# Recurrent mixer with its heads in pairs: values of two heads as one moving operand, outputs of two heads together

## The reference

```python
def _hgrn2_mixer(h, w_in, lb, out_gain, w_out):
    q, f_logit, i, g = jnp.split(h @ w_in, 4, axis=-1)
    log_f = jnp.log(lb + (1.0 - lb) * jax.nn.sigmoid(f_logit))
    k = (1.0 - lb) * jax.nn.sigmoid(-f_logit)
    ...
    _, o = lax.scan(_hgrn2_chunk, s0, (qc, kc, vc, gc))   # v is i, decay is log_f
    o = _rmsnorm(o, out_gain)
    o = o * jax.nn.sigmoid(g.astype(jnp.float32))
    return o.astype(h.dtype) @ w_out
```

## Time and profile before

| | |
|---|---|
| median of 3 runs | 1961.22 us (1957.46 to 1961.35) |
| profiled execution | 1960.82 us, its span 1958.8 us |
| PE busy | 1822.2 us, 93% |
| DVE, ACT, POOL busy | 1193.8, 959.9, 528.6 us |
| mean granted PE clock | 0.967 |
| the mixer's stage | about 226 to 430 us |

### The profile page before, as it was taken

How to read it: one execution, slowest core, us unless ns; L and a number is a source line. 1 busy time by engine, 2 the same in 40 slices (tenths; PEclk the granted TensorE clock), 3 DMA queues, 4 the chain that set the end, 5 groups by cost and what they waited for, 6 DMA issues and landing times. The chain is left out here.

```text
span 1958.8 us, 36818 instructions
## 1 busy us (share of the span) xinstructions
PE 1822.2 (93%) x14492; PEld 1787.5 (91%) x14492; DVE 1193.8 (61%) x1716; ACT 959.9 (49%) x1086; POOL 528.6 (27%) x409
## 2 busy tenths in 40 slices
PE   7999989969999899997998999979899998879999
PEld 7999879969999899996998999978799998879998
DVE  6655678866555665555666555564477763337776
ACT  5444667654435653443335444554454554445544
POOL 2001546620004500034664000565400026650001
PEclk9999989979999899998999999989999998889999
DMA  6555323225554445533343555433244543344542
GB/s 220 201 188 215 111 93 122 97 86 193 190 176 170 139 165 185 187 132 110 112 145 109 195 189 182 162 112 111 105 172 174 190 161 108 103 155 151 193 174 105
DMA packets 44877, 298.21 MB, mean 152 GB/s; under 512 B 4992, under 2 KB 5376, under 8 KB 15376
## 3 DMA queue, kind: packets, MB, share of 16 engines
q1 hardware_dynamic: 44816, 297.38, 42.7%
HBM read 296.31 MB, written 1.05 MB: 152 GB/s over the span
## 5 line engine op out<-in xcount | busy, mean ns | idle before, releaser
L2253 POOL TENSOR_TENSOR w_lo<-raw,w_hi 128x512 fp32r<-128x512 f32 (+2 forms) x403 | 527.8, 1342 | 1415.3 <-ACT w_hi L299 1415.1
L299 ACT ACTIVATE w_hi<-raw 128x2048 fp32r<-128x2048 f32 (+5 forms) x298 | 531.7, 1793 | 456.9 <-PE wk L349 374.2
L348 PE MATMUL wk<-x_lo,w_hi 128*128 128x256 f32 x2560 | 732.4, 286 | 0.0
L347 PE MATMUL wk<-x_hi,w_hi 128*128 128x256 f32 x2208 | 637.5, 289 | 27.1 <-DVE x_lo L422 15.8
L349 PE MATMUL wk<-x_hi,w_lo 128*128 128x256 f32 x2208 | 631.4, 286 | 0.0
L319 DVE TENSOR_TENSOR w_lo<-raw,w_hi 128x2048 fp32r<-128x2048 f32 x180 | 411.7, 2290 | 160.7 <-ACT w_hi L299 160.7
L348 PEld LDWEIGHTS wk<-x_lo,w_hi 128*128 128x128 f32 x2560 | 498.6, 195 | 0.4
L347 PEld LDWEIGHTS wk<-x_hi,w_hi 128*128 128x128 f32 x2208 | 430.8, 195 | 31.0 <-DVE x_lo L422 16.6
L349 PEld LDWEIGHTS wk<-x_hi,w_lo 128*128 128x128 f32 x2208 | 430.1, 195 | 0.0
L347 PE MATMUL acc<-h_hi,w_hi 128*128 128x256 f32 x1376 | 392.6, 285 | 33.5 <-DVE h_lo L2167 10.8
L348 PE MATMUL acc<-h_lo,w_hi 128*128 128x256 f32 x1376 | 387.8, 282 | 0.0
(11 more groups left out here) (294 smaller groups left out, 2258.3 us busy)
## 6 DMA issues: line engine op xcount, KB each, us to landing
raw<-w_ffn_loop SPq DMA_DIRECT2D x120, 1024.0 KB, 4.8
raw<-w_conv_loop SPq DMA_DIRECT2D x60, 1024.0 KB, 4.8
raw<-w_mla_loop SPq DMA_DIRECT2D x18, 768.0 KB, 4.2
raw<-w_hgrn_loop SPq DMA_DIRECT2D x12, 896.0 KB, 4.5
raw<-w_ple_gate SPq DMA_DIRECT2D x8, 1024.0 KB, 4.8
raw<-w_odd_loop SPq DMA_DIRECT2D x10, 768.0 KB, 4.2
raw<-w_ffn_first SPq DMA_DIRECT2D x6, 1024.0 KB, 4.8
raw<-w_even_loop SPq DMA_DIRECT2D x6, 1024.0 KB, 4.8
```

Of the source, the lines that this page charges most:

```text
L299: nc.scalar.activation(w_hi[slot][:, 0:n], raw[slot][:, 0:n], ACT.Copy).then_inc(S("hi_ready"), 1)
L347: nc.tensor.matmul(dst, hi, a_hi, start=start, stop=False, skip_group_check=True)
L348: nc.tensor.matmul(dst, hi, a_lo, start=False, stop=False, skip_group_check=True)
L2253: last = nc.gpsimd.tensor_tensor(w_lo[slot][:, a:b], raw[slot][:, a:b], w_hi[slot][:, a:b].bitcast(F32), ALU.subtract)
```

## The change

Heads are worked in pairs. The values of heads 2r and 2r+1 are projected together: `value_tiles` moves two weight tiles side by side (256 columns), 6 matmuls for two tiles. For PE and DVE there are now two bodies. The **odd** one (i = 1, 3, 5) projects f, q and g of head i+1 ahead of round a, and the values of the pair (i+1, i+2) in two halves, one behind round a and one behind round b; it has no output tiles. The **even** one (i = 2, 4, 6) projects f, q ahead of round a and g behind it, has no value tiles, and does the output tiles of both heads of the last pair, 16, behind round b. The first body has g, the first pair's values are projected ahead of it. `h_val`, `h_hi`, `h_lo`, `hg_g` and `hg_v` hold two heads. On DVE `gate` stands ahead of the gathers in the first and the odd bodies, and at the end, behind the wait for `o`, in the even ones. Units: `proj0` 40 tiles (14, 14, 12), `proj1` 24 (12, 12), a turn of the loop 80 tiles for two heads in 6 units (five of 14, one of 10).

```diff
-    def hgrn_proj(h):
-        t = [("a_w_in", k, c * D + h * P) for k in range(KD) for c in (1, 0)]
-        return t + [("a_w_in", k, c * D + h * P) for c in (3, 2) for k in range(KD)]
+    def hgrn_gates(h):
+        return [("a_w_in", k, c * D + h * P) for k in range(KD) for c in (1, 0)] + [("a_w_in", k, 3 * D + h * P) for k in range(KD)]
+
+    def hgrn_values(h):
+        return [("a_w_in", k, 2 * D + (h + n) * P) for k in range(KD) for n in range(2)]
+
+    def hgrn_out(h):
+        return [("a_w_out", h, n * P) for n in range(KD)]
...
-            mixer(name, A_HEADS, hgrn_proj, lambda h: [("a_w_out", h, n * P) for n in range(KD)],
-                  (3, 11), (3, 14), (1, 8))
+            add(name + ".proj0", 1, 3, 14, lambda i: hgrn_gates(0) + hgrn_values(0))
+            add(name + ".proj1", 1, 2, 12, lambda i: hgrn_gates(1))
+            add(name + ".loop", A_HEADS // 2 - 1, 6, 14, lambda r: hgrn_gates(2 * r + 2) + hgrn_values(2 * r + 2) + hgrn_gates(2 * r + 3)
+                + hgrn_out(2 * r) + hgrn_out(2 * r + 1))
+            add(name + ".out0", 1, 1, 8, lambda i: hgrn_out(A_HEADS - 2))
+            add(name + ".out1", 1, 1, 8, lambda i: hgrn_out(A_HEADS - 1))
...
-        HG_V_VALUES = Steps("hgrn_values", "v", "gate")
+        HG_V_VALUES = Steps("hgrn_pair_values", "v")
+        HG_V_GATE = Steps("hgrn_gates", "gate")
...
+            g_tiles = x_tiles(wk[:, 1, 0:SEQ], True)
+
+            def value_tiles(bank):
+                return x_tiles(lambda b: wk[:, bank, b * SEQ:b * SEQ + SEQ], True, tokens=True)
+
+            def body(i, kind, seg=None, first=0, pair=None):
+                has_next, has_last = kind != "last", kind != "first"
                 if has_next:
-                    use_tiles(pe, *seg, 0, f_q[:8])
+                    use_tiles(pe, *seg, first, f_q[:8])
                 if has_last:
                     mean(i - 1)
                 if has_next:
-                    use_tiles(pe, *seg, 8, f_q[8:], "hgrn_f_q_done", 15)
-                if has_next and not has_last:
-                    HG_V_VALUES.after(pe, i, "gate")
-                    use_tiles(pe, *seg, 16, x_tiles(wk[:, 1, 0:SEQ], True) + token_x)
+                    use_tiles(pe, *seg, first + 8, f_q[8:], "hgrn_f_q_done" if kind != "even" else None, first + 15)
+                if kind in ("first", "odd"):
+                    HG_V_GATE.after(pe, i, "gate")
+                    use_tiles(pe, *seg, first + 16, g_tiles, "hgrn_g_done" if kind == "odd" else None, first + 23)
                 HG_V_PREP.after(pe, i, "scaled")
                 if has_last:
                     HG_V_OUT.after(pe, i - 1, "normed")
+                else:
+                    HG_V_VALUES.after(pe, pair, "v")
                 round_(i, 0)
-                if has_next and has_last:
-                    HG_V_VALUES.after(pe, i, "gate")
-                    use_tiles(pe, *seg, 16, x_tiles(wk[:, 1, 0:SEQ], True) + token_x)
+                if kind == "odd":
+                    HG_V_GATE.after(pe, i + 1, "gate")
+                    use_tiles(pe, *seg, first + 24, value_tiles(1)[:4], wide=2)
+                elif kind == "even":
+                    HG_V_VALUES.after(pe, pair, "v")
+                    use_tiles(pe, *seg, first + 16, g_tiles)
                 if has_next:
                     HG_V_PREP.after(pe, i + 1, "q")
                 else:
                     HG_V_GATHER.after(pe, i - 1, "across")
                 HG_P_SCORES.done(nc.tensor.matmul(wk[:, 0, 0:P], kt[:, LEVELS, 0:P], qt[:, LEVELS, P:SEQ], start=True, stop=True,
                                                   skip_group_check=True), "across")
-                if not has_next:
+                if kind == "last":
                     HG_V_OUT.after(pe, i - 1, "lo")
                     use_tiles(pe, out0, 0, 0, out_tiles(1))
                 HG_V_GATHER.after(pe, i, "a3")
                 round_(i, 1)
-                if has_last and has_next:
+                if kind == "odd":
+                    use_tiles(pe, *seg, first + 32, value_tiles(1)[4:], wide=2)
+                elif kind == "even":
                     HG_V_OUT.after(pe, i - 1, "lo")
-                    use_tiles(pe, *seg, 32, out_tiles(1))
+                    use_tiles(pe, *seg, first + 24, out_tiles(2))
                 HG_V_GATHER.after(pe, i, "b3")
-                HG_V_VALUES.after(pe, i, "v")
-                nc.tensor.matmul(wk[:, 2, 0:SEQ], hg_v[:, 0:P], hg_st[:, 0:SEQ], start=True, stop=False, skip_group_check=True)
-                HG_P_O.done(nc.tensor.matmul(wk[:, 2, P:SEQ], hg_v[:, P:SEQ], hg_st[:, SEQ:384], start=False, stop=True,
+                HG_V_VALUES.after(pe, pair, "v")
+                v0, v1 = (hg_v[:, c:c + P] for c in ((0, SEQ) if kind in ("first", "even") else (P, SEQ + P)))
+                nc.tensor.matmul(wk[:, 2, 0:SEQ], v0, hg_st[:, 0:SEQ], start=True, stop=False, skip_group_check=True)
+                HG_P_O.done(nc.tensor.matmul(wk[:, 2, P:SEQ], v1, hg_st[:, SEQ:384], start=False, stop=True,
                                              skip_group_check=True), "o")
...
-            body(0, has_last=False)
+            use_tiles(pe, proj0, 0, 24, value_tiles(2), wide=2)
+            body(0, "first", (proj1, 0), pair=0)
             with pe.Fori(0, loop.n) as r:
-                body(r + 1)
-            body(A_HEADS - 1, has_next=False)
+                body(r * 2 + 1, "odd", (loop, r), 0, pair=r)
+                body(r * 2 + 2, "even", (loop, r), 40, pair=r + 1)
+            body(A_HEADS - 1, "last", pair=A_HEADS // 2 - 1)
             mean(A_HEADS - 1)
             HG_V_OUT.after(pe, A_HEADS - 1, "lo")
-            last_outputs(pe, out1, 1)
+            hs = out_tiles(2)[KD:]
+            for b in range(4):
+                use_tiles(pe, out1, 0, 2 * b, hs[2 * b:2 * b + 2], "acc_done" if b < 3 else None, 2 * b + 1)
...
+            def hi(i, slot, r):
                 HG_V_OUT.after(act, i, "y")
-                need(act, "unit_used", out_used("hgrn", i))
-                HG_A_OUT.done(nc.scalar.activation(h_hi[:, 0, :], h_val[:, 0, :], ACT.Copy), "hi")
+            def body(i, slot, r):
                 rms(i - 1)
                 sigmoids(i + 1)
-                out_sigmoid(i)
+                out_sigmoid(i, slot)
                 log_f(i + 1)
-                hi(i - 1)
-                round_next(act, loop, i - 1, 0)
+                hi(i - 1, 1 - slot, r)
+                k = 0 if slot else 3
+                round_next(act, loop, r, k)
                 decays(i + 1)
-                round_next(act, loop, i - 1, 1)
+                round_next(act, loop, r, k + 1)
                 square(i)
-                round_next(act, loop, i - 1, 2)
+                round_next(act, loop, r, k + 2)
+
+            def bodies(r):
+                body(r * 2 + 1, 1, r)
+                body(r * 2 + 2, 0, r)
...
-            def value_gate(i):
+            def values(bank):
                 for b in range(TB):
-                    last = nc.vector.tensor_scalar(hg_v[:, b * P:b * P + P], wk[:, 1, SEQ + b * P:SEQ + b * P + P],
+                    last = nc.vector.tensor_scalar(hg_v[:, b * SEQ:b * SEQ + SEQ], wk[:, bank, b * SEQ:b * SEQ + SEQ],
                                                    rstd_tok[:, 2 * b:2 * b + 1], None, ALU.mult)
                 HG_V_VALUES.done(last, "v")
-                HG_V_VALUES.done(mul(hg_g, wk[:, 1, 0:SEQ], rstd[:, :]), "gate")
+
+            def gate(i, slot):
+                HG_A_OUT_GATE.after(v, i - 2, "sigmoid")
+                HG_V_GATE.done(mul(tiles(hg_g, 2)[:, slot, :], wk[:, 1, 0:SEQ], rstd[:, :]), "gate")
 
...
-            def body(i, has_next=True, has_last=True):
+                HG_V_OUT.done(nc.vector.tensor_tensor(h_lo[:, slot, :], h_val[:, slot, :], h_hi[:, slot, :].bitcast(F32), ALU.subtract), "lo")
+            def body(i, kind, r=None):
+                has_next, has_last = kind != "last", kind != "first"
+                slot = 1 if kind in ("odd", "last") else 0
                 if has_last:
                     normed(i - 1)
+                if kind == "first":
+                    v.wait_ge(S("hgrn_f_q_done"), 1)
+                elif kind == "odd":
+                    v.wait_ge(S("hgrn_f_q_done"), r + 2)
+                elif kind == "even":
+                    unit_done(v, loop, r, 3)
                 if has_next:
                     f(i + 1)
                 if has_last:
-                    y(i - 1)
+                    y(i - 1, 1 - slot)
                     HG_P_O.after(v, i - 1, "o")
-                if not has_next:
-                    lo(i - 1)
+                if kind == "last":
+                    lo(i - 1, 1 - slot)
+                if kind == "first":
+                    unit_done(v, proj1, 0, 1)
+                    gate(i + 1, 1 - slot)
+                elif kind == "odd":
+                    v.wait_ge(S("hgrn_g_done"), r + 1)
+                    gate(i + 1, 1 - slot)
                 gather(i, 0)
```

(18 more changed lines are left out.)

52 lines of the change are left out of this document (22 added, 30 removed).

## The result

| | before | after |
|---|---|---|
| median | 1961.22 us (1956.19 to 1975.05, 9 runs) | 1979.83 us (1978.56 to 1984.31, 9 runs) |
| span of the profiled execution | 1958.8 us | 1978.0 us |
| mean granted PE clock | 0.967 | 0.959 |

A forecast was written before the change was run, and what follows sets the result against it. The loop was taken as bound by a closed chain through PE's f/q tiles, DVE's long preparation and the outputs. Terms 4.8 + 0 + 6.0 + 3.0 + 0.9 + 0.4 = +15.1 us on 1960.8 gave 1975.9 us, range 1964 to 1982.

The forecast's parts named there:

- The values are cover, nothing of PE's 19 us comes through: Loop of heads: value matmuls run beside DVE's longer chain, so PE's 19 us less work saves no time.
- Even body 25.3, odd body 23.35: Loop bodies without clock loss: even ones 1.9 us longer than 23.4, odd ones unchanged; +4.8 us together.
- Waits of 5.9 and 3.8 us: PE idles 5.9 us for `lo` in even bodies and 3.8 us for the last gather in odd ones.
- Clock +9.0: Matmuls at 1.2 GHz behind PE's loop waits: +6.0 us in even bodies, +3.0 us in odd ones.
- First body +0.9: First body: a larger POOL unit delays `scaled` and round a runs at 1.2 GHz, +0.9 us.
- End of the stage before +0.4: End of the feed-forward before: ACT rounds 14 tiles for 11 ahead of a waiting activation, POOL a chunk more, +0.4 us.
- Last body 0, rest 0: Last body stays as it was, its waits being ACT's and DVE's; no change was forecast behind it either.
- the chain without the clock: Rival in the loop: longer chain as forecast, but PE's clock stays at 2.4 GHz; 1966 us, chance 0.13.
- POOL missing DVE: Rival in the loop: POOL's run misses DVE's subtractions, waits shrink, clock stays up; -13 us, 1948 us, chance 0.10.

The follow-up runs named there:

- e7: Kernel before with two thirds of each value tile's matmuls left out (256 fewer): 1961.66 us, ratio 1.0012 to before.
- e2: Changed kernel with zero matmuls in PE's loop waits, 14 in odd bodies and 26 in even ones: 1974.56 us, ratio 1.0079 to before.
- e3: Changed kernel with `lo` on DVE moved ahead of the preparation of the next head: 1974.27 us, ratio 1.0075 to before.
- e4: Changed kernel with `g` behind round a in odd bodies too, all values behind round b, `gate` behind first gathers and `q`: 1979.85 us, ratio 1.0112 to before.
- e5: Changed kernel with the edits of e1, e3 and e4 together: 1961.85 us, ratio 1.0021 to before.
- e1: Changed kernel with ACT's rounding of `proj1`'s last unit in the opening moved behind the norm's rstd: 1973.05 us, ratio 1.0072 to before.
- e10: Kernel before with zero matmuls only in PE's waits of the first and last body: 1954.68 us, ratio 0.9981 to before.

## Why the prediction was right

The forecast was 1975.9 us, range 1964 to 1982, slower with 0.82; measured 1979.83. Step by step:

- **The values are cover, nothing of PE's 19 us comes through.** Right; e7 shows it apart from everything else.
- **Even body 25.3, odd body 23.35.** With the clock out of the way e2 has 25.6, 25.5, 25.4 and 23.3. `lo` behind the preparation is what the even body waits for: e3 moves it and the wait is gone. Body 6 was taken at +1.0 for its smaller POOL units; without the fillers' overrun it costs +1.4, and its wait is the shorter one (4.31 us). In the odd body `f` (325.22) to the first gather (329.88) is 4.66 us (forecast 4.74) and from there to the end of the last gather (341.34) 11.46 (forecast 11.6): POOL's run meets the gathers first, as forecast. Chain: 4.8 forecast, 5.7 measured.
- **Waits of 5.9 and 3.8 us.** Measured 5.87, 5.88 and 4.31 before the outputs, 3.86 to 3.88 before `o`.
- **Clock +9.0.** e2 says 9.2 with its overrun and 10.6 without. The sum was nearly right, its places were not: all three even bodies carry it, since the odd bodies' wait is followed by the even bodies' f/q tiles. A wait of 3.8 us in the odd body was enough for it, and so were shorter ones: in e4 and e5 the clock fell behind 3.2 and 2.6 us too.
- **First body +0.9.** Measured +0.95, and by the forecast's steps: PE waits 4.43 us before round a (forecast 4.6), which then takes 3.5 us.
- **End of the stage before +0.4.** The step that failed: +5.8. Of the second unit's larger size only ACT's and POOL's own time was counted, not **what ACT waits for** before it may overwrite the buffer. e1, which takes away the wait (4.53 us) together with the rounding, gets the 5.5 us back.
- **Last body 0, rest 0.** -0.9 and -3.4. The first term I can't assign. The second can't be called an effect of the change: the last column of the table has the same work in thirteen kernels and spreads from 1518.5 to 1524.7 us, and executions of the kernel before alone differ by some 6 us. Where in these stages PE's clock stands on arrival may be the reason, but no run here isolates it. So the nearness of 1975.9 to 1979.8 is in part luck: 8.4 us were missed on one side (5.4 in the opening, 3.0 in the loop, of which 1.6 clock, 0.9 chain and 0.5 the first body), and 4.3 given back on the other.

The rivals: the chain without the clock falls with e2. POOL missing DVE falls with the 1.35 us subtractions above, still there.

## What to carry to other kernels

Before taking work off the busiest engine, close the loop of waits by hand: if the removed work lies beside another engine's longer chain, it is cover, and its absence costs twice, once as a wait and again as a slow clock behind it; the cheap probe is to leave part of that work out and look (e7). When a unit of a streamed buffer grows, ask for each rounding or load that reuses the buffer which consumer it now waits for, and what stands behind it on its own engine (e1). A wait on PE that can't be removed can be filled with matmuls of zeros, ahead of the waiting step (e10), and no longer than the shortest wait of the loop: in e2 26 of them fit two bodies and cost the third 1.4 us.
